# Attention with a Hyena filter beside it, one core: score banks of their own for each map, and the value product moved into the next turn's first half

## The reference, cut to what matters

```python
def _diff_scores(q, k, v, lam):
    """q (B,Q,H,2,d), k (B,K,H,2,d), v (B,K,H,2d) -> (B,Q,H,2d)."""
    s = jnp.einsum('bqhmd,bkhmd->bhmqk', q, k).astype(F32) * DIFF_SCALE
    p = jax.nn.softmax(s, axis=-1)
    attn = p[:, :, 0] - lam * p[:, :, 1]
    return jnp.einsum('bhqk,bkhe->bqhe', attn.astype(v.dtype), v)
```

## Time and profile before

| what | us |
|---|---|
| time, median of 3 runs | 3829.0 (3826.55 to 3842.98) |
| the profiled execution: its time | 3828.31 |
| the profiled execution: its span | 3826.5 |
| busy over the span: PE, DVE, ACT, POOL | 3363.5, 2391.5, 1088.9, 1065.3 |
| row maxima (line 1727), 144 instructions: busy | 197.4 |
| idle of DVE just before them | 115.9 |
| exp (line 1609), 144 instructions: busy | 177.2 |
| mean granted clock of TensorE | 0.953 of 2.4 GHz |

### The profile page before, as it was taken

One profiled execution on the slowest core, in us unless ns is written; L12 is line 12 of the kernel. 1 busy time (PEld: TensorE's weight loads), 2 busy tenths in 40 slices (PEclk: granted clock), 3 DMA queues, 4 the chain that ended last, 5 costly groups with the idle time before them and its releaser, 6 DMA issues. The chain is left out here.

```text
span 3826.5 us, 48036 instructions
## 1 busy us (share of the span) xinstructions
PE 3363.5 (88%) x18212; PEld 2736.8 (72%) x18212; DVE 2391.5 (62%) x3952; ACT 1088.9 (28%) x1980; POOL 1065.3 (28%) x766
## 2 busy tenths in 40 slices
PE   6999999999968885886997888999999588858698
PEld 2788888888758784654783576888888588845477
DVE  4134566765459986885554324557865489968765
ACT  2112222212245554332211211222221355523321
POOL 4233334333202322210122423433443022232121
PEclk8999999999979998998998899999999799989899
DMA  5354223223173222334426155323332633133441
GB/s 205 72 157 149 81 93 96 89 90 91 54 211 100 79 69 99 114 106 137 155 77 220 50 121 170 98 76 94 100 100 74 202 92 94 44 109 112 130 151 64
DMA packets 414889, 423.30 MB, mean 111 GB/s; under 512 B 57040, under 2 KB 351440, under 8 KB 413506
## 3 DMA queue, kind: packets, MB, share of 16 engines
q1 hardware_dynamic: 368676, 315.22, 28.5%
q10 hardware_dynamic: 45984, 105.01, 7.8%
HBM read 287.76 MB, written 124.01 MB: 108 GB/s over the span
## 5 line engine op out<-in xcount | busy, mean ns | idle before, releaser
L763 PE MATMUL l_p_acc<-l_u_hi,l_w_hi 128*128 128x512 f32 (+1 forms) x2208 | 605.8, 376 | 25.6 <-ACT l_p_stg L827 10.8
L763 PE MATMUL l_p_acc<-l_u_hi,l_w_lo 128*128 128x512 f32 (+1 forms) x2208 | 587.3, 367 | 0.0
L763 PE MATMUL l_p_acc<-l_u_lo,l_w_hi 128*128 128x512 f32 (+1 forms) x2208 | 586.4, 367 | 0.0
L763 PEld LDWEIGHTS l_p_acc<-l_u_hi,l_w_hi 128*128 128x128 f32 x2208 | 383.6, 189 | 102.5 <-issue 28.7
L676 POOL TENSOR_TENSOR l_w_hi<-l_wt,l_p_zero 128x1024 fp32r<-128x1024 f32 x100 | 199.6, 1996 | 916.4 <-PE l_p_acc L763 762.0
L763 PEld LDWEIGHTS l_p_acc<-l_u_hi,l_w_lo 128*128 128x128 f32 x2208 | 380.9, 189 | 71.7
L763 PEld LDWEIGHTS l_p_acc<-l_u_lo,l_w_hi 128*128 128x128 f32 x2208 | 380.5, 188 | 71.7
L1493 PE MATMUL l_at_pS<-l_at_k_hi,l_at_q 128*128 128x512 f32 (+1 forms) x400 | 165.8, 415 | 125.3 <-ACT l_at_prob L1609 69.9
L678 POOL TENSOR_TENSOR l_w_lo<-l_wt,l_w_hi 128x1024 fp32r<-128x1024 f32 x100 | 267.7, 2677 | 7.8
L1727 DVE TENSOR_REDUCE l_at_nmax<-l_at_pS 128x1 f32<-128x1280 f32 (+1 forms) x144 | 197.4, 1371 | 115.9 <-PE l_at_pS L1494 113.7
L2444 PE MATMUL l_o_pA<-l_o_w_hi,l_o_o_hi 128*128 128x512 f32 x576 | 223.6, 407 | 43.1 <-DVE l_o_o_lo L2554 31.2
(11 more groups left out here) (321 smaller groups left out, 6932.2 us busy)
## 6 DMA issues: line engine op xcount, KB each, us to landing
l_wt<-w_in SPq DMA_DIRECT2D x104, 512.0 KB, 3.9
l_n_wa<-w_ada SPq DMA_DIRECT2D x10, 2048.0 KB, 16.6
kf_d<-l_p_R SPq DMA_DIRECT2D x72, 256.0 KB, 3.7
xbc_d<-l_p_fin ACTq DMA_DIRECT2D x28, 640.0 KB, 3.0
l_at_K<-kf_d SPq DMA_DIRECT2D x64, 256.0 KB, 2.9
l_o_rows<-w_out SPq DMA_DIRECT2D x32, 512.0 KB, 4.5
l_o_oT<-o_d SPq DMA_DIRECT2D x16, 1024.0 KB, 6.8
qk_d<-l_p_late ACTq DMA_DIRECT2D x12, 1280.0 KB, 4.6
```

Source lines behind the costliest of these rows:

```text
L763: mm = pe.matmul(acc[:, a:a + w], (w_hi, w_lo)[wp][m % 2][:, k], (u_hi, u_lo)[up][:, k, t0 + c:t0 + c + w], start=(k == n == 0), stop=(k = ...
```

## The change

Each map gets three banks of its own (`MAP = 3 * BANK`), so the scores take six banks. The bank `pO` goes away: the value product now lies in the unused columns of map 1's last bank. The last pieces of the scores no longer wait for the other map's exp; map 1's last piece waits until the older output in its bank has been scaled, and `values` waits until the exp of map 1 of the unit before the current one has read that bank. On PE, `scores(i, 0)` comes first in a turn, then `values(i - 3)` (the product of a unit moves from the end of one turn to the start of the next), then the first `turn`. On ACT, `exp(i, 0)` comes first, then `norm(i - 3)`, then the three copies in a row.

```diff
-        pS = ps(nc, ctx, tag + "pS", 5 * BANK)
+        pS = ps(nc, ctx, tag + "pS", 6 * BANK)
+        pO = pS[:, 5 * BANK + CTX:5 * BANK + CTX + P]
         pT = ps(nc, ctx, tag + "pT", BANK)
-        pO = ps(nc, ctx, tag + "pO", BANK)
         pH = ps(nc, ctx, tag + "pH", BANK)
+        MAP = 3 * BANK
...
-                    pieces = [(0, CTX)] if q < CT else [(0, BANK), (BANK, BANK), (2 * BANK, CTX)] if m == 0 else [(CTX, BANK), (CTX + BANK, BANK), (0, CTX)]
-                    for c, w in pieces:
-                        out = pS[:, m * T + c:m * T + c + w]
-                        if w == CTX and q >= CT and n + m:
-                            pe.wait_ge(exped, 2 * n + m)
+                    for c, w in [(0, CTX)] if q < CT else [(0, BANK), (BANK, BANK), (2 * BANK, CTX)]:
+                        out = pS[:, m * MAP + c:m * MAP + c + w]
+                        if m == 1 and c == 2 * BANK and n >= 3:
+                            pe.wait_ge(scaled, n - 2)
...
+                    pe.wait_ge(exped, 2 * min(n + 3, NU))
+                    pe.wait_ge(turned_copied, before[n + 1])
                     for kt in range(keys(q) // P):
-                        if kt % 4 == 0:
-                            pe.wait_ge(turned_copied, before[n] + kt // 4 + 1)
-                        mm = pe.matmul(pO[:, 0:P], mixT[:, kt], v_s[:, h % 2, kt], start=(kt == 0), stop=(kt == keys(q) // P - 1))
+                        mm = pe.matmul(pO, mixT[:, kt], v_s[:, h % 2, kt], start=(kt == 0), stop=(kt == keys(q) // P - 1))
...
                     turning = batches[i - 2] if 2 <= i < NU + 2 else 0
+                    if i < NU:
+                        scores(i, 0)
+                    if 3 <= i < NU + 3:
+                        values(i - 3)
                     if turning > 1:
                         turn(i - 2, 0, False)
-                    if i < NU:
-                        scores(i, 0)
                     if n is not None:
                         forward(n)
...
                         turn(i - 2, turning - 1, i >= 4)
-                        values(i - 2)
...
+                    if i < NU:
+                        exp(i, 0)
+                    if 3 <= i < NU + 3:
+                        norm(i - 3)
                     if turning > 1:
                         copy(i - 2, 0)
-                    if 3 <= i < NU + 3:
-                        norm(i - 3)
                     if turning > 2:
                         copy(i - 2, 1)
-                    if i < NU:
-                        exp(i, 0)
                     if turning:
                         copy(i - 2, turning - 1)
```

More of the change, by code:

```diff
@@ L1608, in exp @@
                         act.wait_ge(mixed, n + m - 1)
-                    act.activation(prob[:, (2 * n + m) % 3, 0:keys(q)], pS[:, m * T:m * T + keys(q)], ACT.Exp,
+                    act.activation(prob[:, (2 * n + m) % 3, 0:keys(q)], pS[:, m * MAP:m * MAP + keys(q)], ACT.Exp,
                                    bias=nmax[:, n % 2, m:m + 1], accum_out=sums[:, n % 4, m:m + 1]).then_inc(exped, 1)
@@ L1620, in norm @@
                     act.activation(small_sq[:, n % 2:n % 2 + 1], sums[:, n % 4, 0:1], ACT.Square, scale=math.sqrt(RMS_EPS)).then_inc(squared, 1)
-                    act.activation(junk[:], pO[:, 0:P], ACT.Square, accum_out=ss[:, n % 2:n % 2 + 1]).then_inc(squared, 1)
+                    act.activation(junk[:], pO, ACT.Square, accum_out=ss[:, n % 2:n % 2 + 1]).then_inc(squared, 1)
                     act.wait_ge(squared, 2 * n + 2)
@@ L1628, in norm @@
                         act.wait_ge(o_turned, n - 1)
-                    act.activation(o_t[:, n % 2], pO[:, 0:P], ACT.Copy, scale=rms[:, n % 2, 1:2]).then_inc(scaled, 1)
+                    act.activation(o_t[:, n % 2], pO, ACT.Copy, scale=rms[:, n % 2, 1:2]).then_inc(scaled, 1)
                 def copy_rows(n):
@@ L1726, in maximum @@
                     dve.wait_ge(scored, 2 * n + m + 1)
-                    dve.tensor_reduce(nmax[:, n % 2, m:m + 1], pS[:, m * T:m * T + keys(q)], AX.X, ALU.max, negate=True).then_inc(maxed, 1)
+                    dve.tensor_reduce(nmax[:, n % 2, m:m + 1], pS[:, m * MAP:m * MAP + keys(q)], AX.X, ALU.max, negate=True).then_inc(maxed, 1)
                 def combine(n):
```

## The result

The changed kernel takes 3935.1 us (median, 3919.3 to 3940.6) against 3830.1 us (3826.6 to 3843.0) in the same series: the ratio is 1.0253 (95% interval 1.0229 to 1.0277), so it is 2.5% slower. The forecast was 3897 us in a range of 3850 to 3950. The profiled execution took 3940.6 us, the longest of its four, of which 3938.8 are its span.

A forecast was written before the change was run, and what follows sets the result against it. DVE was taken to set the pace. From 3828.3 us, +61 us (full turns 56, short turns 8, layer starts and ends -3) and +8 us for PE's clock gave 3897 us, range 3850 to 3950.

The forecast's parts named there:

- DVE sets the pace: In the steady turns DVE bounds the kernel: busy 40.30 of 42.70 us in four turns.
- PE's 1.07 us is off the path: Map 1's last score piece waits 1.07 us for map 0's exp; hidden under DVE's work, worth nothing by itself.
- The second halves lose their 1.85 us: From max1 to the next max0, DVE's waits of 0.84 and 1.01 us in four turns go away.
- that turn's fixed length: The first of four steady turns takes 6.71 us from max0 to max1 both before and after the change.
- The chain of 6.70 us: From max0 to max1: step to exp, exp, norm, copy, transposes, scores; 6.70 us, adding 6.2 us in four turns.
- The value product "is no part of it": The moved value product, 2.24 us on PE, ends early enough not to lengthen the new path from max0 to max1.
- Turns with `turn_rows`: Transposes wait for DVE's gate; max1 to max0 takes 5.5 us or DVE's own time; +1.1 us a turn.
- The clock: PE's idle gaps of 2.0 to 3.6 us sometimes halve its clock: +8 us; falling in every turn, +78 us, chance 0.10.
- One in ten: Share of turns in which PE's clock was taken to fall, between never (0) and always (78 us).
- The short turns of layer 0: 14 turns where the scored or transposed unit is short: between 0 and 1.1 us each, taken as 0.6, 8 us.
- The sum: Full turns 56 us, short turns 8, layer starts and ends -3: +61 us, and +8 for PE's clock.
- starts: At each layer's start the freed last piece gives back up to 1 us; with the ends, -3 us for both layers.

The follow-up runs named there:

- experiment 11: Changed kernel's banks, PE's old order, value product beside map 0's last piece, ACT's rows' copy ahead of norm and exp of map 1: 3832.6 us, ratio 0.9983.
- experiment 9: Changed kernel's banks, PE's old order, value product beside map 0's last piece, norm at the end of ACT's turn: 3845.7 us, ratio 1.0030.
- experiment 5: Changed kernel with ACT's first copy ahead of the norm, exp of map 0 still ahead of both: 3882.3 us, ratio 1.0126.
- experiment 4: Changed kernel with eight extra 128x512 filler matmuls in PE's gap, in full turns from the 14th on: 3926.0 us, ratio 1.0239.
- experiment 1: Changed kernel with ACT's old order put back, banks and PE's order as changed: 3870.6 us, ratio 1.0089.
- experiment 6: Kernel before with PE's new order alone; its five shared banks, own pO bank and ACT's old order stay: 3927.3 us, ratio 1.0238.
- experiment 7: Changed kernel with POOL's 1024-column products cut to 128 columns: 3926.4 us, ratio 1.0243.

## Why the prediction was right in direction and short in size

*DVE sets the pace; PE's 1.07 us is off the path.* Right for max1, wrong for the late max0. DVE's first halves hide the wait. But in the earlier trace rows PE never stands still from the end of the wait, at 3200.84 us, to the max0 at 3207.38, for which DVE waits 0.84 us: last piece, value product, backward step, transposes and scores follow without a gap. So the wait is one of the things that make the 1.85 us, and only the move of the value product was credited with them. What it is worth by itself no run shows. In experiment 11 map 1's last piece waits for no exponential and four turns win 0.05 us, but there a wait of the value product and the slower combination took back what was freed. That kernel with POOL's product cut was not run.

*The second halves lose their 1.85 us.* They did: 4.78, 4.62, 6.13 and 5.04 us without idle time, where I had 4.79, 4.47, 6.13 and 4.89. What I left out is what else waited in that idle time. The combination of the turn with POOL's 1024-column product had taken 2.45 us in the kernel before because DVE was 1.01 us late. Now it starts earlier and overlaps the product longer. Other kernels lie between: 0.60 us late and 2.87 us in experiment 9, 0.43 and 3.02 in experiment 11, 0.14 and 3.27 in the changed kernel. The timelines of the kernel before, POOL's product and DVE's combination:

```profile
3186.62 2.38 POOL L1677 TENSOR_TENSOR l_at_hu<-l_at_hu,l_at_hx 128x1024 f32<-128x1024 f32 x1
```

```profile
3187.90 2.45 DVE L1739 SCALAR_TENSOR_TENSOR l_at_mix<-l_at_prob,l_at_back 128x1280 f32<-128x1280 f32 x1
```

and POOL's product of the changed kernel, to the combination of 3.27 us at 3268.14 shown above:

```profile
3267.72 2.35 POOL L1678 TENSOR_TENSOR l_at_hu<-l_at_hu,l_at_hx 128x1024 f32<-128x1024 f32 x1
```

Before, 3189.00 - 3187.90 = 1.10 us of the combination lay beside the product, and it was 2.45 - 1.55 = 0.90 us longer than one alone. Now it is 1.93 us and 1.72 us: the combination does next to nothing while the product runs. Of the 1.01 us of idle time, 0.84 were given back in the same turn. The Trainium skill, SBUF — State Buffer (section Who interferes with whom), says that a DVE instruction with two inputs in SBUF contends with a GpSimd instruction that reads SBUF; the numbers here agree. I had taken 6.71 us as that turn's fixed length. The trace of before held a warning that I passed over: layer 0 has one such turn of 7.55 us already, and its longest combination took 3.29 us. In 12 of the 52 full turns, those with such a product, the first halves lie 7.5 us over the forecast, most of it for this reason. (A thirteenth, turn 37 of layer 0, does not belong here: its combination is 2.91 us in both kernels, and max1 comes 3.36 us late from PE, at a low clock.)

*The chain of 6.70 us.* Right, link by link: 6.74 to 6.75 us at full clock in every turn where the chain ended the half, and without the norm it is 1.31 us shorter (experiment 5). With 6.70 us in each first half and the second halves as measured, the 52 full turns come to +58.4 us against the forecast's 56. The mean period of four turns is 12.59 us, not 11.8; at full clock (experiment 4) it is 12.10, and of the 0.3 left 0.22 are the combination's.

*The value product "is no part of it".* For the full turns of the changed kernel this held: the chain on ACT is longer than PE's list. As a statement on the edit it was misleading. Take the chain away and the moved value product is the next limit (experiment 1), +38 us with the contention. It was hidden cost, not absent cost.

*Turns with `turn_rows`.* Second halves of 5.39 to 5.47 us, forecast 5.5, and 6.13 where DVE's own work is longer; the eight turns grew by 9.2 us, 1.15 each, forecast 1.1.

*The clock.* Forecast one fall in ten turns and +8 us. Over the chain's 6.70 us, the first halves of the other 40 full turns have 17.1 us too much; 2 of them are the 0.05 us by which the chain was short, and about 15 are the clock's: 14 of the 52 full turns, by 0.3 to 1.5 us each. Experiment 4 gives 12.1 us for the turns that have filler. What failed is the frequency. Of the last 16 turns of layer 1, six have a first half that only the clock explains (7.60, 8.18, 7.32, 8.16, 7.04 and 7.48 us): the four with gaps of 2.94 to 3.29 us, which is every turn behind a second half of 6.13 us, and two with gaps of 1.87 and 1.86 us, while another gap of 1.87 us did nothing. "One in ten" came from two rows and was a guess. The gaps were off too: forecast 2.0 to 3.6 us, in those 16 turns 0.80 to 3.29. The Trainium skill's rule that I weighed (TensorE: Matmul & The Clock Gate, section A second HAM failure mode: psum-queue depth-cycling) has the clock swing between groups of matmuls; the trace agrees that it does, in six turns of 16.

*The short turns of layer 0.* I took 14 x 0.6 = 8 us; the trace has +20.2 us. In 12 of the turns it is 0.94 us each, near the upper bound that I had set. The last two, 38 and 39, bring 8.8 us: their first halves grew from 2.31 and 1.35 us to 8.56 and 5.74. A wait that I had costed at nothing stands there, in PE's timeline:

```profile
1524.94 4.10 PE L1525 MATMUL l_at_pS<-l_at_v,l_at_mixT 128*128 128x128 f32 x20 [2.50 <-ACT l_at_prob L1610]
```

The value product waits 2.50 us for the exp of map 1, because it shares a bank with map 1's last piece, and then takes 4.10 us in place of 2.4. No long second half lies ahead of it here, which would have covered the wait; I had argued from steady turns. ACT's order is not the cause: in experiment 1 these two first halves are 8.51 and 6.12 us. In experiment 6, where both engines keep the order of experiment 1 and the product has a bank of its own, they are 5.35 and 4.36. There the product of turn 38 takes 4.05 us as well, but it waits 0.33 us and starts 0.75 us before max0; in the changed kernel it starts 1.44 us after it. So about 4.9 us go with the shared bank, mostly by the wait.

*The sum.* In the stages the trace has +83.0 (full turns) + 20.2 (short) - 0.6 (starts) = +102.6 us, where I had 69. The other 9.7 us of the profiled executions' 112.3 lie outside, in code that the change does not touch (+9.2 before the first maximum of layer 0, -5.7 between the layers, +6.1 at the end): I take it for scatter of single executions. No term failed by sign; those mis-sized are the combination (7.5 against 0), the short turns (20.2 against 8) and the clock (about 15 against 8).

## What to carry to other kernels

The wait that meets the eye first in a profile (PE, 1.07 us) can be worth less than the order that removes it costs, when that order puts six links in front of the engine that sets the pace; write down each of that engine's next starts and every link up to it before moving anything. When idle time is removed, ask what it had kept apart: here it held a DVE instruction out of the way of a POOL one, and the versions that won the idle time and kept that whole product paid it back. In an in-order queue the place of one short copy, ahead of the norm or behind it, was worth 53 us (experiment 5); put first what another engine waits for, and behind it what nobody waits for soon (the norm).

## What was not expected of the hardware

More work made the kernel shorter: 8 matmuls of 128x512 in a gap of 3.3 us took 7.06 us from four turns, by a granted clock of 1.00 in place of 0.85. The length of one standstill did not decide whether the clock fell: behind 1.87 us it did in one turn and not in another, and in experiment 7 turns 16 and 24 of layer 0 kept a granted clock of 1.00 behind 3.29 and 3.31 us (first halves of 6.74 and 6.76 us). And the interference of DVE and POOL is nearly exclusive: a combination of 1.55 us took 3.27 us beside a product of 2.35 us.
